# Rope halves of two heads in one query product; key weights issued ahead of the last state stores

## What is computed

```python
def _mla_project(p_mla, pos, p):
    cq = p_mla[..., :Q_RANK]                                  # 512
    q = (_rmsnorm(cq, p['q_norm']) @ p['w_q_up']).reshape(B, T, 8, 128 + 64)
    q_rope = _rope(q[..., 128:], pos)                         # x*cos + turned(x)*sin, 64 wide
    q_lat = jnp.einsum('bthn,rhn->bthr', q[..., :128], p['w_uk'])   # 256 wide
    ...
# attention: scores = (q_lat . latent + q_rope . krope) * scale, softmax, context in latent form
# prompt: causal over 256 keys; each sequence: 2048 cached keys in 16 pages of 128, and 4 new ones
```

## Time and profile before

| | us |
|---|---|
| three runs | 1924.51, 1926.02, 1920.31 (median 1924.51) |
| the profiled execution | 1916.01, of which the span is 1914.0 |
| busy in the span | PE 1750.1, DVE 1137.2, ACT 302.3, POOL 329.7 |
| mean granted TensorE clock | 0.947 of full |
| load of the constants at the start, 1112.5 KB | 5.3 to landing |
| query weights, 1920 and 1152 KB | 8.6 and 6.3 to landing |
| key weights, value weights, 1024 KB each | 5.1 and 7.2 to landing |
| a latent page, 128 KB; a page of rope keys, 32 KB | 2.1 and 1.8 to landing |

### The profile page before, as it was taken

The page is one execution under the profiler, slowest core; times in us unless marked ns, Lnnn a source line. Parts: engine busy times, 40 slices in busy tenths (PEclk is TensorE's granted clock), DMA queues, the critical chain, the costliest instruction groups (busy, mean ns, idle before and its releaser), DMA issues.

```text
span 1914.0 us, 39377 instructions
## 1 busy us (share of the span) xinstructions
PE 1750.1 (91%) x15968; PEld 1544.2 (81%) x15968; DVE 1137.2 (59%) x1635; ACT 302.3 (16%) x742; POOL 329.7 (17%) x459
## 2 busy tenths in 40 slices
PE   4869999999999799779994999999999999999995
PEld 2359999776667466556894999999999999999994
DVE  0147676455454364335778776666766776666776
ACT  0030001332222124323003100000000000000003
POOL 0000100133333134302215320001000110011113
PEclk9679999999999799879996999999999999999997
DMA  9996554766754725347352454555554555555421
GB/s 332 352 298 203 163 175 135 270 218 225 273 194 151 257 73 152 88 123 237 101 164 88 125 157 160 176 152 159 176 171 145 171 176 160 153 173 166 152 80 50
DMA packets 289394, 333.61 MB, mean 174 GB/s; under 512 B 36019, under 2 KB 235220, under 8 KB 288532
## 3 DMA queue, kind: packets, MB, share of 16 engines
q1 hardware_dynamic: 286242, 325.32, 52.7%
q10 hardware_dynamic: 940, 3.82, 0.6%
q0 software_dynamic: 2048, 2.10, 0.4%
HBM read 323.63 MB, written 7.57 MB: 173 GB/s over the span
## 4 chain that ended last, share of the span: by engine, by line
PE 77%; SPq 7%; DMA 6%; DVE 5%; issue 3%; ACT 1%; POOL 0%; ACTq 0%; DVEq 0%
PE bank L1239 20%; PE bank L1241 20%; PE bank L1240 20%; DMA slab<-in_w_ada_dram 6%; SPq L457 4%; PE bank L1297 3%; SPq L454 2%; PE bank L1492 2%; DVE xT L2350 1%; PE bank L1479 1%; PE bank L1198 1%; PE bank L1210 1%; PE bank L1705 1%; PE bank L1187 1%; PE bank L1804 1%
## 5 line engine op out<-in xcount | busy, mean ns | idle before, releaser
L1239 PE MATMUL bank<-arena_hi 128*128 128x288 f32 (+1 forms) x2864 | 854.1, 298 | 37.3 <-DVE hT_lo L1893 27.7
L1241 PE MATMUL bank<-arena_hi,slab_lo 128*128 128x288 f32 (+1 forms) x2864 | 846.3, 295 | 0.0
L1239 PEld LDWEIGHTS bank<-arena_hi 128*128 128x128 f32 (+1 forms) x2864 | 539.0, 188 | 44.7 <-DVE hT_lo L1893 25.0
L1240 PE MATMUL bank<-hT_lo,arena_hi 128*128 128x288 f32 (+2 forms) x1840 | 546.9, 297 | 0.0
L1241 PEld LDWEIGHTS bank<-arena_hi,slab_lo 128*128 128x128 f32 (+1 forms) x2864 | 541.8, 189 | 0.0
L2290 DVE TENSOR_TENSOR slab_lo<-slab,arena_hi 128x2048 fp32r<-128x2048 f32 x144 | 351.5, 2441 | 5.0
L1240 PEld LDWEIGHTS bank<-hT_lo,arena_hi 128*128 128x128 f32 (+2 forms) x1840 | 348.4, 189 | 0.2
L2289 DVE CAST arena_hi<-slab 128x2048 fp32r<-128x2048 f32 x144 | 176.8, 1228 | 273.6 <-PE bank L1241 262.0
L1240 PE MATMUL bank<-arena_hi 128*128 128x288 f32 x1024 | 302.1, 295 | 0.0
L1240 PEld LDWEIGHTS bank<-arena_hi 128*128 128x128 f32 x1024 | 192.3, 188 | 0.0
L798 POOL TENSOR_TENSOR arena<-arena 128x288 f32<-128x288 f32 x64 | 67.8, 1059 | 650.6 <-ACT arena L1144 650.6
(11 more groups left out here) (360 smaller groups left out, 1939.8 us busy)
## 6 DMA issues: line engine op xcount, KB each, us to landing
slab<-in_w_ada_dram SPq DMA_DIRECT2D x48, 2048.0 KB, 9.1
slab<-in_w_up_dram SPq DMA_DIRECT2D x32, 2048.0 KB, 9.4
slab<-in_w_down_dram SPq DMA_DIRECT2D x32, 2048.0 KB, 8.3
slab<-in_w_in_dram SPq DMA_DIRECT2D x16, 2048.0 KB, 8.5
slab<-in_cache_latent_dram SPq DMA_DIRECT2D x128, 128.0 KB, 2.1
slab<-in_w_out_dram SPq DMA_DIRECT2D x8, 2048.0 KB, 9.2
x_park<-xT SPq DMA_DIRECT2D x1, 2304.0 KB, 13.6
xT<-x_park SPq DMA_DIRECT2D x1, 2304.0 KB, 12.7
```

The lines of the kernel that those rows point to most:

```text
L1239: pe.matmul(b[0:w, 0:NTOK], w_hi[:, k, 0:w], x_hi[:, k, :], start=(k == 0), stop=False)
L1240: pe.matmul(b[0:w, 0:NTOK], w_hi[:, k, 0:w], x_lo[:, k, :], start=False, stop=False)
L1241: mm = pe.matmul(b[0:w, 0:NTOK], w_lo[:, k, 0:w], x_hi[:, k, :], start=False, stop=(k == KT - 1))
```

## The change

The query weights are loaded by kind and not by head: the no-rope columns of all eight heads into slab 3 and the rope columns into slab 0, as four DMAs each (one per 128 rows of the weight), with pieces of 512 and 256 bytes. The rope columns of heads 2p and 2p + 1 stand side by side, so one product of 128 rows makes both; its odd head lies on partitions 64 to 127. One rotation (a product with a 128 x 128 matrix that holds the 64 x 64 one twice) and one `rotate` of 128 partitions do both heads. cos and sin are kept on all 128 partitions, the rotated key of the prompt too, and the scores of odd heads read the upper halves. GpSimd gathers the rope queries of the sequences in four copies instead of two.

TensorE makes the no-rope product of head 0 and the rope product of pair 0 before it turns the key weights. On SP the key weights are issued ahead of the last pair's state stores, behind the same waits.

```diff
-C_CAUS = C_ROT + 64
+C_CAUS = C_ROT + 128
...
-        slab_free[QUP], slab_free[QUP + 1] = (q_mm, 5), (q_mm, MH)
+        slab_free[QUP], slab_free[QUP + 1] = (q_mm, 12), (q_mm, 11)
...
-            for n, (h0, nh) in enumerate(((0, 5), (5, 3))):
+            qup = a["mla_w_q_up"][0].rearrange("(k p) (h c) -> k p h c", p=P, c=QH)
+            for n, (c0, w) in enumerate(((0, NOPE), (NOPE, ROPE))):
                 sp.wait_ge(ada_mm, N_ADA + N_LATE - 1 + n)
-                sp.dma_start(quv[n][:, :, 0:nh * QH], qup[:, :, h0 * QH:(h0 + nh) * QH]).then_inc(slab_in[(QUP + n) % RING], 16)
-            states_out(PAIRS - 1)
+                for k in range(4):
+                    sp.dma_start(ring[(QUP + n) % RING][:, k * MH * w:(k + 1) * MH * w].rearrange("p (h c) -> p h c", h=MH),
+                                 qup[k, :, :, c0:c0 + w]).then_inc(slab_in[(QUP + n) % RING], 16)
             s = WUK % RING
             wait_free(WUK)
             sp.wait_ge(e_t, 12 * PAIRS)
             sp.dma_start(ring[s][:, 0:2 * MH * NOPE].rearrange("p (k c) -> p k c", k=2),
                          a["mla_w_uk"][0].rearrange("(k p) h n -> p k (h n)", p=P)).then_inc(slab_in[s], 16)
+            states_out(PAIRS - 1)
             sp.wait_ge(state_out, 16 * 9 * PAIRS)
...
-            pool.tensor_copy(krT[0:64, :], mla[0:64, 6, :]).then_inc(lat_kept, 1)
+            ch.link(pool.tensor_copy(krT[0:64, :], mla[0:64, 6, :]))
+            pool.tensor_copy(krT[64:128, :], mla[0:64, 6, :]).then_inc(lat_kept, 1)
+            pool.wait_ge(lat_kept, 1)
...
             for h in range(MH):
-                act.wait_ge(q_mm, h + 1)
+                act.wait_ge(q_mm, nope_count(h))
                 if h >= 2:
                     act.wait_ge(ql_mm, h - 1)
-                    act.wait_ge(qr_ready, h - 1)
-                act.activation(qn[:, h % 2, :], bank[h % 2][:, 0:NTOK], ACT.Copy)
-                act.activation(qraw[0:64, h % 2, :], bank[2][0:64, 0:NTOK], ACT.Copy).then_inc(q_copied, 1)
+                act.activation(qn[:, h % 2, :], bank[h % 2][:, 0:NTOK], ACT.Copy).then_inc(q_copied, 1)
+                if h % 2 == 0:
+                    pair = h // 2
+                    act.wait_ge(q_mm, rope_count(pair))
+                    if pair >= 2:
+                        act.wait_ge(qr_ready, pair - 1)
+                    act.activation(qraw[:, pair % 2, :], bank[2][:, 0:NTOK], ACT.Copy).then_inc(q_copied, 1)
...
+            up_nope(0)
+            up_rope(0)
             pe.wait_ge(slab_in[WUK % RING], slab_ready(WUK))
...
             for h in range(MH):
                 if h + 1 < MH:
-                    up_project(h + 1)
-                pe.wait_ge(q_copied, h + 1)
-                if h:
-                    pe.wait_ge(qr_ready, h)
-                pe.matmul(bank[4][0:64, 0:NTOK], rot, qraw[0:64, h % 2, :], start=True, stop=True).then_inc(q_rot, 1)
+                    up_nope(h + 1)
+                if h % 2 and h + 1 < MH:
+                    up_rope(h // 2 + 1)
+                if h % 2 == 0:
+                    pe.wait_ge(q_copied, rope_count(h // 2))
+                    if h:
+                        pe.wait_ge(qr_ready, h // 2)
+                    pe.matmul(bank[4][:, 0:NTOK], turn, qraw[:, h // 2 % 2, :], start=True, stop=True).then_inc(q_rot, 1)
+                pe.wait_ge(q_copied, nope_count(h))
...
-                pe.matmul(b, qrT[0:64, h, tok], krT[0:64, 0:nk], start=True, stop=False)
+                half = slice(h % 2 * 64, h % 2 * 64 + 64)
+                pe.matmul(b, qrT[half, h // 2, tok], krT[half, 0:nk], start=True, stop=False)
...
             for h in range(MH):
-                dve.wait_ge(q_rot, h + 1)
-                if h:
-                    dve.wait_ge(qr_ready, h)
-                rotate(qrT[0:64, h, :], qraw[0:64, h % 2, :], bank[4][0:64, 0:NTOK], [rot_a, rot_b], qr_ready)
+                if h % 2 == 0:
+                    dve.wait_ge(q_rot, h // 2 + 1)
+                    if h:
+                        dve.wait_ge(qr_ready, h // 2)
+                    rotate(qrT[:, h // 2, :], qraw[:, h // 2 % 2, :], bank[4][:, 0:NTOK], [rot_a, rot_b], qr_ready)
```

More of the change, by code:

```diff
@@ L86, in shape_constants @@
     ang = (pos[None] * inv[:, None]).astype(np.float32)
-    for q in range(2):
+    for q in range(4):
         t[32 * q:32 * q + 32, C_COS:C_COS + NTOK] = np.cos(ang)
@@ L90, in shape_constants @@
     for m in range(32):
-        t[m + 32, C_ROT + m] = -1.0
-        t[m, C_ROT + 32 + m] = 1.0
+        for e in (0, 64):
+            t[e + m + 32, C_ROT + e + m] = -1.0
+            t[e + m, C_ROT + e + 32 + m] = 1.0
     t[:, C_CAUS:C_CAUS + P] = np.where(c <= r, 0.0, NEG)
@@ L311, in build @@
         qlT = qlT.rearrange("p (r h) n -> p r h n", r=2)
-        qrT, o = carve(o, MH, NTOK)
+        qrT, o = carve(o, MH // 2, NTOK)
+        o += MH // 2 * NTOK
         latT, o = carve(o, 2, NTOK)
```

70 lines of the change are left out of this document (39 added, 31 removed).

## The result

| | us |
|---|---|
| before, four runs | median 1925.26 (1920.31 to 1930.49) |
| after, four runs | median 1954.91 (1951.12 to 1958.27) |
| ratio | 1.0153, 95% interval 1.0119 to 1.0187 |
| profiled execution after, its span | 1953.43, 1951.8 |

The account below looks back on a forecast made before the run. It took SP's one-by-one issuing of cache pages as the bound of the attention; +0.95, +0.4, +0.6 and +0.1 made +2.05, say +2.0 us, and on the median of 1924.5 gave 1926.5 us, range 1920 to 1933.

Parts of the forecast that it names:

- What bounds the attention: From 660.44 us on, SP's one-by-one issuing of 192 cache-page DMAs, some 0.98 us each in the long groups, sets the pace.
- the query stage worth 0: The query stage ends some 15 us earlier, but SP's issuing covers it, so 0 on the path.
- Rival A: TensorE's gain in the query stage arrives, less what unit 1 takes: 1912 us; chance 5%.
- the wait before unit 4: TensorE's idle time for latent pages in the attention, 10.9 us before the change, becomes about 20.
- The terms ahead of the first page: On SP's path to the first cache page: +0.95 for the first store, +0.4 for eight stores, +0.6 for the prompt store.
- the first state store: In SP's queue, it goes out behind the key weights at about 653.9 instead of 652.96: +0.95 us.
- The eight stores: SP's sample-state stores now run beside weight loads: +0.4 us (0 to 0.8).
- The prompt store: The prompt-state store, with key weights ahead of it, lands in 2.8 us instead of 2.17: +0.6 (0 to 1.5).
- Eight loads in small pieces: SP issues the query weights' eight DMAs by 652.8, just inside 653.2: 0, with little to spare.
- Rival B: The query weights' pieces hold up SP's stores between 643 and 662, up to 2.6 ns each: +13, 1937.5 us; chance 15%.
- Constants: The table loaded at the start of the span grows by 64 columns of 2225: +0.1 us.
- Key weights landing by 660: Issued ahead of the state stores, the key weights land at about 659 to 660 us instead of 664.1.

Follow-up runs that it names:

- e9: The change's compute alone: changed kernel with 3 KB pieces, state stores ahead of the key weights and 20 dummy products; ratio 1.0030 to the kernel before.
- lean pair: Changed compute and kernel before, both with rope keys of units 4 and 5 on GpSimd, value weights and six small stores issued later: 0.9808 and 0.9885.
- padded: The changed kernel plus 20 tiny dummy products on TensorE ahead of the feed-forward loop: ratio 1.0013, measured again 1.0032.
- e10: The kernel before with only the key weights issued ahead of the last pair's state stores: ratio 1.0007.
- e13: The kernel before with only the change's larger table of constants (64 columns more): ratio 1.0005.
- after + 50: The changed kernel plus 50 dummy products on TensorE ahead of the feed-forward loop: 1935.91 us, ratio 1.0055.

## Why the prediction was wrong

- **What bounds the attention, and the query stage worth 0: right.** With SP as the bound nothing of the shorter stage arrived (e9); with SP relieved 11.7 of 17.2 us did, and 13 in the lean pair. Rival A is out. The stage itself gained more than forecast (15, 10 to 16): 17.7 us in this profile, 18.0 between the means of five profiles after and six before; one part of it is that two heads take 10.2 us and not 11.2. The gain did not go where it was expected: the wait before unit 4 went from 10.9 to 8.8 and not to 20, that before unit 1 is 11.1, rope keys take 8 us more, and the rest is the clock. In e9 page waits grew by 9.8 us, and the same products took 165.1 us at a granted clock of 0.86, not 156.2 at 0.91.
- **The step that failed was left out of the sum.** The prediction took the rope halves as 0 on the path and all stages behind the attention as they were; that fewer products also make the program shorter had no term. TensorE's program got 78 instructions shorter, the loop head moved from 66 to 244 in its block, and three passes lost 22.6 us in the timed runs. Neither the forecast nor a rival named it, so the range, 1920 to 1933, could not hold 1954.9. The trace of before did show the place: three idle times without a releaser at the loop head. The sum did not ask why they were there and what could make them longer.
- **The terms ahead of the first page: +1.95 forecast, +4.2 measured.** In five profiles of the changed kernel, padded or not, the first state store goes out 12.4 to 12.9 us behind the first load of the query weights, where it was 10.0 (+2.7, forecast +0.95). The eight stores take 5.5 to 7.3 us against 5.25 (mean +0.9, forecast +0.4). The prompt store lands after 2.35 to 3.94 us against 2.17 (mean +0.7, forecast +0.6; in e10, with the key weights alone moved, it was 0). So the largest miss lies in front of the stores, where the loads in small pieces were put at 0.
- **Eight loads in small pieces: 0 forecast.** SP was to be through 8.8 us behind the first issue (644 to 652.8), and it took 11.2 to 12.0. The prices per piece were near: with the DMA engines full 300 GB/s moved from 648.0 to 653.5, 1.7 ns for 512 bytes as forecast, and 185 to 201 GB/s from 654.5 to 657.5, which is 1.3 to 1.4 ns for 256 bytes and not 1.13. What the sum lacked is the start: the first issue is at 644.96, and from 645.5 to 646.5 the engines' share is only 0.17. The rest of the 3 us, the dearer short pieces and fewer than 2500 of them in flight, no run separates. SP's issues of 1.6 to 2.1 us each, 1.6 to 2.0 ns a piece, fall in the time in which the engines were full. Rival B's mechanism did occur and its threshold of 1.5 ns was passed; its upper price of 2.6 ns and its +13 us were too high.
- **The Trainium skill on short pieces** ("DMA: Bandwidth & Descriptors", Specifications) has the loss begin under 512 bytes. Here the pieces of 512 bytes are already slow: 296 to 302 GB/s in three profiles with the engines full, where pieces of 2 KB had 412, and 182 to 201 for those of 256 bytes.
- **Constants: +0.1, none that can be seen** (e13: +1.0 us in the means, interval -4 to +6). Key weights landing by 660: wrong, they came 8.6 us after their issue, at 665.5, behind the pieces. It cost nothing, since TensorE had the first two query products to do.
- Without the stall the changed kernel is at 1.0013 and 1.0032 of before; 1.001 was forecast. That this is near is in part luck: the distances in the profiles say 7.6 us for the output product, the timed runs 3.3 and 5.4; which is nearer stays open.

## What to carry to other kernels

Before costing an edit that lengthens or shortens an engine's program, look for idle times without a releaser at the heads of its loops behind the edit: the runs tie them to the jump, and where the head stands in its block of 256 instructions decides whether a second and larger one follows. Pad by a few idle instructions until the head has enough work left in its block (here some 9 us of products, an estimate from the twelve stops of 6.1 to 9.2 us), or write the loop out on every engine that has it, since the stall of one hides that of another. And where one queue's issuing is the bound, a shorter compute stage pays only after work has been moved off that queue. Compare stages by their distance from a mark ahead of them and not by the clock of two executions, which here lay up to 16 us apart.

## What was unexpected in the hardware

- A jump back costs TensorE 1.4 to 2.0 us, and 4.1 to 6.9 us more if the block of the loop head has only 12 to 14 instructions left; with 68 left 1.0 to 2.9, with 186 to 190 none. VectorE's jump costs 5.7 to 8.3 us in the same loop, beside TensorE's products.
- After such a stop of 8 us TensorE resumed at the lower clock: for some 3 us its products came every 0.24 us and not every 0.13 (granted clock 0.73 as the mean of 1280 to 1290 us). In after + 50 it did so once behind a jump alone, idle for 1.9 us (1480.99).
- DMAs with 1024 pieces, issued back to back, cost SP mostly 1.6 to 2.1 us each from the third on, whether a piece has 512 or 256 bytes, while the DMA engines were full and moved 300 GB/s; two DMAs with 512 pieces of 3 KB were out in 5.6 us, the wait between them included.
